# Seven more weight chunks of a three-block transformer done as seven half-size products instead of eight

## The reference, cut to what matters

```
# block one
proj = x @ w_in_a;  u = gelu(proj[:, :768]);  gv = layer_norm(gelu(proj[:, 768:1536]));  qm = proj[:, 1536:]
mix = u * (w_s @ gv + b_s);   att = concat(mix, memory_attention(qm, mk, mv)) @ w_out_a
# block two
q = x @ w_in_b[:, :768];  k = x @ w_k_shared;  v = x @ w_v_shared
# block three
h = rmsnorm(x);  rq, rk, rv, rg, nq, nk, nv, xq, gates = split(h @ w_in_2)
# each expert block
y += ((silu(t @ w_gate[e]) * (t @ w_up[e])) @ w_down[e]) * gate[e]
```

## Time and profile before

| what | us |
|---|---|
| median of three runs | 1697.32 |
| profiled execution, its device time | 1697.71 |
| span of the profiled execution | 1696.0 |
| PE busy | 1648.3 (97%) |
| VectorE busy | 448.9 (26%) |
| ScalarE busy | 288.5 (17%) |

### The profile page before, as it was taken

The page is one execution under the profiler, slowest core; times in us unless marked ns, Lnnn a source line. Parts: engine busy times, 40 slices in busy tenths (PEclk is TensorE's granted clock), DMA queues, the critical chain, the costliest instruction groups (busy, mean ns, idle before and its releaser), DMA issues.

```text
span 1696.0 us, 20423 instructions
## 1 busy us (share of the span) xinstructions
PE 1648.3 (97%) x8806; PEld 940.5 (55%) x8806; DVE 448.9 (26%) x940; ACT 288.5 (17%) x584; POOL 62.4 (4%) x92
## 2 busy tenths in 40 slices
PE   9999999999899999999999999899999999999997
PEld 7784433433333685644344333348787888866654
DVE  1470000000000225300000000025266657722222
ACT  2301101101011222111011000012222122321212
POOL 4000000000000100000000000005000000000000
PEclk9999999999999999999999999999999999999999
DMA  9889999999999955999999999999254445699996
GB/s 335 324 323 375 429 427 428 427 428 428 425 426 428 386 200 216 354 427 428 427 429 426 428 427 427 428 406 330 95 199 149 151 147 198 251 401 425 425 424 284
DMA packets 88491, 597.46 MB, mean 352 GB/s; under 512 B 6104, under 2 KB 17104, under 8 KB 54208
## 3 DMA queue, kind: packets, MB, share of 16 engines
q1 hardware_dynamic: 84768, 586.30, 85.4%
q0 software_dynamic: 3616, 9.65, 1.8%
HBM read 594.88 MB, written 1.05 MB: 351 GB/s over the span
## 4 chain that ended last, share of the span: by engine, by line
PE 59%; issue 26%; DMA 12%; DVE 2%; POOL 1%; ACT 0%; POOLq 0%; DVEq 0%
PE psum L952 31%; PE psum L658 8%; DMA ring<-in_w_gate_dram 8%; PE psum L645 4%; DMA ring<-in_w_up_dram 4%; PE psum L935 3%; PE psum L602 3%; PE psum L1046 2%; PE psum L652 1%; PE psum L893 1%; PE psum L1085 1%; PE psum L1062 1%; POOL rstd L3339 1%; PE psum L780 1%; PE psum L594 1%
## 5 line engine op out<-in xcount | busy, mean ns | idle before, releaser
L952 PE MATMUL psum<-ring,xT 128*64 128x512 f32 (+1 forms) x2020 | 416.4, 560 | 29.5 <-DMA ring<-in_w_up_dram 11.2
L952 PEld LDWEIGHTS psum<-ring,xT 128*64 128x64 f32 x2020 | 144.5, 137 | 272.7 <-issue 243.8
L952 PE MATMUL psum<-ring,work 128*64 128x512 f32 x992 | 220.1, 593 | 0.8 <-DMA ring<-in_w_down_dram 0.7
L2615 DVE TENSOR_TENSOR work<-work,psum 128x512 f32<-128x512 f32 (+1 forms) x45 | 41.0, 910 | 573.9 <-PE psum L952 568.3
L952 PEld LDWEIGHTS psum<-ring,work 128*64 128x64 f32 x992 | 70.7, 137 | 136.6 <-issue 131.3
L645 PE MATMUL psum<-xT,ring 128*128 128x256 f32 x512 | 113.6, 380 | 0.0
L1925 ACT COPY work<-psum 128x512 f32<-128x512 f32 (+1 forms) x45 | 23.2, 515 | 488.9 <-PE psum L1062 488.9
L658 PE MATMUL psum<-ring,mkv 128*128 128x256 f32 x456 | 104.9, 380 | 0.0
L645 PEld LDWEIGHTS psum<-xT,ring 128*128 128x128 f32 x512 | 96.3, 190 | 13.8 <-issue 0.8
L658 PE MATMUL psum<-ring,xT 128*128 128x256 f32 x400 | 92.0, 379 | 0.3 <-issue 0.3
L658 PEld LDWEIGHTS psum<-ring,mkv 128*128 128x128 f32 x456 | 85.7, 190 | 11.8 <-DVE work L3188 0.3
(11 more groups left out here) (378 smaller groups left out, 1647.2 us busy)
## 6 DMA issues: line engine op xcount, KB each, us to landing
ring<-in_w_gate_dram SPq DMA_DIRECT2D x48, 2048.0 KB, 20.5
ring<-in_w_down_dram SPq DMA_DIRECT2D x48, 2048.0 KB, 22.1
ring<-in_w_up_dram SPq DMA_DIRECT2D x48, 2048.0 KB, 21.8
ring<-in_w_in_dram SPq DMA_DIRECT2D x16, 2048.0 KB, 11.4
ring<-in_w_exp_up_dram SPq DMA_DIRECT2D x15, 2048.0 KB, 19.1
work<-in_w_gate_dram SPq DMA_DIRECT2D x10, 2048.0 KB, 14.5
ring<-in_w_exp_down_dram SPq DMA_DIRECT2D x10, 2048.0 KB, 20.4
work<-in_w_exp_gate_dram SPq DMA_DIRECT2D x9, 2048.0 KB, 15.0
```

The source lines that it names most:

```text
L952: ins = pe.matmul(to[part * CAP:(part + 1) * CAP, 0:n], lhsT=lhsT, rhs=w[:, half * n:(half + 1) * n], start=first, stop=last)
L2615: dve.tensor_tensor(by_rows(h[:, 0:F], j), in_order(silu[:, 0:F], j), in_order(u_bank[:, 0:F], j), ALU.mult).then_inc(sem("h"), 1)
```

## The change

The tokens and weights of seven more chunks are multiplied with the seven products: `VALUES_A` (512 columns of `gv`) and `INNER_A` (512 columns of `u`) in block one, `QUERY_D` and `KEYS_D` in block two, `QUERY_X`, `QUERY_N` and `KEYS_N` in block three. The first is natural, the other six are turned (`TURNED`). A turned product is eight matmuls of 128 columns where a natural one is four of 256. Blocks one and two get token sums and a scratch block of their own. PE's, ScalarE's and VectorE's lists are laid out anew around them; the order of the weight stream on SyncE is the same. The norm of the second memory is moved behind the keys of block two. The decays are computed at the start of the second expert stage. The join of the cross attention is split into four tiles between other work. Lines that only name things anew are left out.

```
+        TURNED = (INNER_A, QUERY_D, KEYS_D, QUERY_X, QUERY_N, KEYS_N)
+        seven_scale = {QUERY_D: -HD ** -0.5, QUERY_X: -P ** -0.5, QUERY_N: -HD ** -0.5}
+            def partial(b, at, tokens, weights, first=False, turned=False):
+                for f in range(2 if turned else 0):
+                    for c in range(4):
+                        ins = pe.matmul(b[:, f * P:(f + 1) * P], lhsT=weights[:, c, f * P:(f + 1) * P], rhs=tokens[:, c, :], start=first and f == c == 0, stop=(c == 3), skip_group_check=True)
+                for c in range(0 if turned else 4):
                     ins = pe.matmul(b[:, at:at + 256], lhsT=tokens[:, c, :], rhs=weights[:, c, :], ...
...
             # PE, block one
             two_turned(w[:, :, 256:512], xT, DC, 0, "a", "qm")
+            gated_values = first(n + 1)
             freed[n] = nat(w[:, :, 0:256], xT, DC, 256, "a", "gv", pack=True); n += 1
+            second(gated_values)
             scores(att_0, 0, q, keys)
-            tile(w, xT, DC, 512, 0, "a", "gv")
+            sixth_to_fifth(gated_values)
             scores(att_0, 1, q, keys)
             turn_weights(att_0, 0)
-            freed[n] = tile(w, xT, DC, 512, 1, "a", "gv"); n += 1
+            third(gated_values)
+            freed[n] = fourth(gated_values); n += 1
+            inner = first(n)
             scores(att_0, 2, q, keys)
             turn_weights(att_0, 1)
-            two_turned(w, xT, DC, 0, "a", "u")
+            second(inner)
+            sixth_to_fifth(inner)
             scores(att_0, 3, q, keys)
             values(att_0, 0, v)
             turn_weights(att_0, 2)
-            freed[n] = two_turned(w, xT, DC, 1, "a", "u"); n += 1
+            third(inner)
+            freed[n] = fourth(inner); n += 1
             turn_weights(att_0, 3)
...
             # PE, block two
             scores(att_m, 0, q, keys)
-            two_turned(w, xT, DC, 0, "a", "qkv")
+            query = first(n)
             scores(att_m, 1, q, keys)
             turn_weights(att_m, 0)
-            freed[n] = two_turned(w, xT, DC, 1, "a", "qkv"); n += 1
+            second(query)
+            sixth_to_fifth(query)
...
             # PE, block three
+            query = first(n)
+            second(query)
             gate_0 = first(n + 1)
-            freed[n] = two_turned(w, xT, DC, 1, "a", "xa"); n += 1
+            second(gate_0)
+            sixth_to_fifth(query)
+            third(query)
+            freed[n] = fourth(query); n += 1
...
             # ScalarE, block one
+            keep_first_part(VALUES_A)
             weights(att_0, 0)
-            empty(gv[:, 0, 0:512], "gv", ACT.Gelu)
+            keep_part(VALUES_A, 1)
+            keep_part(VALUES_A, 2)
             weights(att_0, 1)
             turn_weights(att_0, 0)
-            empty(gv[:, 1, 0:512], "gv", ACT.Gelu)
+            last_part(VALUES_A, ACT.Gelu)
+            keep_first_part(INNER_A)
+            in_place(VALUES_A, ACT.Gelu, "gv")
...
             # VectorE, block one
+            sum_tokens(VALUES_A)
+            sum_weights(VALUES_A)
+            first_corner(VALUES_A)
             peaks(att_0, 0)
             normal(att_0, 0)
+            other_corner(VALUES_A, 3)
             peaks(att_0, 1)
             normal(att_0, 1)
+            other_corner(VALUES_A, 2)
+            sum_weights(INNER_A)
             peaks(att_0, 2)
             normal(att_0, 2)
+            first_corner(INNER_A)
+            other_corner(INNER_A, 3)
             peaks(att_0, 3)
             output(oT[:, 0, :])
             normal(att_0, 3)
-            dve.wait_ge(S("gv_a"), 3)
+            dve.wait_ge(S("gv_a"), 4)
+            dve.wait_ge(S("last_part"), VALUES_A + 1)
+            other_corner(INNER_A, 2)
             layer_norm(halves(gv, SGW), gv, SGW, 0, (S("prm0_in"), 32))
...
             # VectorE, block two
+            sum_tokens(QUERY_D)
             peaks(att_m, 0)
+            sum_weights(QUERY_D)
             normal(att_m, 0)
-            rms_norm(mem2.__getitem__, mem2.__getitem__, prm[:, 0, 0, :], (S("prm0_in"), 48))
             peaks(att_m, 1)
+            first_corner(QUERY_D)
             normal(att_m, 1)
...
+            other_corner(KEYS_D, 2)
+            rms_norm(mem2.__getitem__, mem2.__getitem__, prm[:, 0, 0, :], (S("prm0_in"), 48))
...
-            expert_layer(1, count)
+            expert_layer(1, count_and_decays)
```

More of the change, by code:

```diff
@@ L1416, in _ @@
             turn_weights(att_m, 2)
-            freed[n] = two_turned(w, xT, DC, 1, "a", "qkv"); n += 1
+            second(keys_d)
+            sixth_to_fifth(keys_d)
             turn_weights(att_m, 3)
+            third(keys_d)
+            freed[n] = fourth(keys_d); n += 1
             two_turned(as_cols(n, 0, 256), xT, DC, 0, "a", "qkv")
@@ L1486, in xa_v @@
                 return mv2[:, k, h * P:(h + 1) * P]
-            second(gate_0)
             wait_made("xa")
+            seven_made(query)
             scores(att_x, 0, xa_q, xa_k)
-            sixth_to_fifth(gate_0)
-            scores(att_x, 1, xa_q, xa_k)
-            turn_weights(att_x, 0)
             third(gate_0)
@@ L1505, in _, with joined @@
             freed[n] = fourth(gate_1); n += 1
-            nq, nk = as_cols(n), as_cols(n + 1)
-            two_turned(nq, xT, DC, 0, "a", "na")
+            scores(att_x, 3, xa_q, xa_k)
+            query = first(n)
+            turn_weights(att_x, 2)
+            second(query)
+            sixth_to_fifth(query)
             turn_weights(att_x, 3)
-            b = bank("a", "na")
-            two_turned_part(nk, xT, DC, 0, b, range(0, 12))
+            third(query)
+            freed[n] = fourth(query)
+            keys = first(n + 1)
             values(att_x, 2, xa_v)
-            full("a", two_turned_part(nk, xT, DC, 0, b, range(12, 16)))
+            second(keys)
+            sixth_to_fifth(keys)
+            def joined(oT, at, half, t):
+                freed[at] = tile(as_rows(at)[:, :, half * 512:(half + 1) * 512], oT, 4, 512, t, "v", "joined")
             def join(oT, at):
-                w = as_rows(at)
                 for half in range(2):
-                    freed[at] = nat(w[:, :, half * 512:(half + 1) * 512], oT, 4, 512, "v", "joined")
+                    for t in range(TC):
+                        joined(oT, at, half, t)
             pe.wait_ge(S("att_o"), att_x.out(2))
-            join(W(XA["oT"], 4, T), n + 2)
+            oT_x = W(XA["oT"], 4, T)
+            joined(oT_x, n + 2, 0, 0)
+            third(keys)
+            freed[n + 1] = fourth(keys)
+            joined(oT_x, n + 2, 0, 1)
             qN, kN, vN = W(NA["qT"], 4, T), W(NA["kT"], 4, T), W(NA["v"], TC, 512)
@@ new lines, in add_product, with first_corner @@
+            def add_product(m, to, b):
+                if m in seven_scale:
+                    dve.scalar_tensor_tensor(out=to, in0=product_of(m, b), scalar=seven_scale[m], in1=to, op0=ALU.mult, op1=ALU.add).then_inc(S("corner"), 1)
+                else:
+                    dve.tensor_tensor(to, product_of(m, b), to, ALU.add).then_inc(S("corner"), 1)
+            def first_corner(m, between=None):
+                n, to, b = sevens[m], seven_to[m][0], bank()
+                dve.wait_ge(S("kept"), 3 * m + 1)
+                add_product(m, to, b)
+                if between is not None:
+                    between()
+                dve.wait_ge(S("weight_sums"), 4 * m + 3)
+                dve.tensor_tensor(block_of(n, 1, 0), block_of(n, 1, 0), sum_at(m), ALU.subtract).then_inc(S("weight_sums"), 1)
@@ L2655, in _, with other_corner @@
+            def other_corner(m, at):
+                if at == 3:
+                    dve.wait_ge(S("a_full"), cornered[m])
+                else:
+                    dve.wait_ge(S("part"), 4 * m + 4)
+                dve.wait_ge(S("kept"), 3 * m + at)
+                add_product(m, seven_to[m][at], RB["a"][(cornered[m] - 1) % BANKS])
             dve.memset(wr_mk[:], 0.0)
@@ L2934, in _, with join_first @@
-            join(XA["gate"])
+            peaks(att_x, 3)
+            sum_weights(QUERY_N)
+            normal(att_x, 3)
+            first_corner(QUERY_N)
+            other_corner(QUERY_N, 3)
+            other_corner(QUERY_N, 2)
+            sum_weights(KEYS_N)
+            output(oT[:, 2:4, :])
+            first_corner(KEYS_N)
+            gate_x = W(XA["gate"], TC, D)
+            def join_first(half, t):
+                cs = slice(half * 512, (half + 1) * 512)
+                dve.wait_ge(S("gate_a"), 2)
+                dve.tensor_tensor(comb[:, t, cs], bank(), gate_x[:, t, cs], ALU.mult).then_inc(S("joined_v"), 1)
```

292 lines of the change are left out of this document (164 added, 128 removed).

## The result

The changed kernel took 1716.81 us (median of 4 runs, 1715.33 to 1720.80), the kernel before 1697.62 us beside it. The ratio is 1.0118, with a 95% interval from 1.0106 to 1.0130. So it is slower by 19.2 us. The forecast was 1702.5 with a range up to 1707.5: the sign was right, the size wrong by a factor of nearly four. The profiled execution is the shortest of the four (1715.33, span 1713.3); against the span of 1696.0 before, the traces have 17.3 us to explain.

A forecast was written before the change was run, and what follows sets the result against it. Expert stages were taken as bound by their weight stream, passing on blocks one and two's lateness, block three by PE. Block one +5.25, two +2.0, three -2.1 gave +5.15 us: 1702.5, own range 1698.5 to 1706, 8-in-10 range 1692.5 to 1707.5.

The forecast's parts named there:

- three forecast pauses: PE waits for the third chunk's landing (2.95 us), before block one's out_second (4.0) and at block two's first softmax (3.9).
- one for one: Blocks one and two: a gain or loss by the block's end is carried whole to its expert stage's end.
- rival 2: The stream swallows blocks one and two's lateness, only block three's -2.1 us counts: 1695.2 us; chance 0.20.
- The PE work removed: All three blocks: VALUES_A saves 1.73 us, six turned chunks 5.8 at 1.835 a product, all seven 7.55.
- (a): Block one: third chunk, wanted earlier in first(n + 1), lands only at 34.3 us; PE stands for 2.95 us.
- (b): Block one: first(inner) waits 0.7 us for a bank, fifth twice 0.15 behind keep_part; 1.0 us in all.
- (c): Block one: gv's layer norm waits behind the last inner corner; 4.0 us of PE idle before out_second.
- Block two's first softmax: Block two: too little work covers the softmax and the weight sums; PE waits 3.9 us at turn_weights(att_m, 0).
- rival 3: The clock drops behind the three new pauses of 3 to 4 us, +2.0 each: 1704.5 to 1708.5; chance 0.15.
- Block three: Block three: products save 2.9 us, two relays cost 0.8 (0.6 and 0.2); -2.1 us in all.
- Rival 1: The waits are hidden on VectorE's list, only the chunk's landing stays: -4.6 us, 1692.7; chance 0.12.
- two decision points: out_second at most 13.1 us behind the inner columns' end (block one); no wait at turn_weights(att_m, 0) (block two).

The follow-up runs named there:

- four repairs: Changed kernel with bank wait split, gv chunk's first product behind packed tile, layer norm ahead of last corner, query tile between block two's scores: 1692.76 us, ratio 0.9975.
- fillers: Changed kernel with products of the identity laid into the four pauses of PE, no wait taken away: 1707.42 us, ratio 1.0054.
- split in the changed kernel: Changed kernel, but at block two's start PE waits for the second token tile's VectorE bank only ahead of that tile's transposes: 1710.52 us, ratio 1.0077.
- fifth repair: The four repairs, plus the second half's two sums of output weights on VectorE moved behind the first mixed tile: 1694.00 us, ratio 0.9984.

## Why the prediction was wrong

Two terms made the difference. The half clock behind the three forecast pauses was put at nothing and carried 7.3 us, and PE's wait at block two's start had no term and cost 6.4.

**What bounds the kernel, right.** The lateness of blocks one and two passed the expert stages but for 0.7 us each, which is within what executions differ by, so "one for one" held and rival 2 (the stream swallows it) fell. The single wait added to the kernel before shows it alone: 4.8 us of idle time and 2.3 of slow records at 570 us are +6.6 us at the end, more than 1,100 us later.

**The PE work removed, too small.** The turned product was priced at 1.835 us from two products that stand alone. Where turned products follow each other it is 1.785 (two from 1235.86 to 1239.43 take 3.57), and each change to another form adds about 0.1 us (two from 616.60 to the `scores` at 620.27 take 3.67). By starts, and without the pauses and the half clock, the turned chunks take 12.8 us for 13.9 in block one, 25.4 for 28.0 in two (four repairs) and 38.1 for 41.6 in three, so they save 7.3 where 5.8 was forecast. `VALUES_A` saves 1.4 where 1.73 was (12.6 for 14.0, four repairs). That is 1.2 us more in all, inside the bounds.

**Block one's waits, two right and one not there.** (a) The landing was forecast for 34.3 and came at 34.36, with PE idle for 2.42 us (forecast 2.95). (b) The 1.0 us for the bank and for `fifth` isn't in the trace: no pause is marked between the landing and 73.39, and `first(inner)` comes 1.87 us behind a product of 1.73. The inner columns ended at 73.39 (forecast 72.6); without the 1.7 us of half clock behind the landing they would have ended 0.9 ahead of the forecast, so that its nearness is luck. (c) The output product starts 17.6 us behind that end (forecast 17.1, before 13.1), and the pause is 4.02 us (forecast 4.0). The run with the norm ahead of the corner shows that their order was the cause.

**Block two's first softmax, right.** 4.07 us for 3.9.

**The term that was mis-sized: the half clock.** The text set it beside the sum ("The sum above has none: most short pauses of this trace leave the clock at 1.00") and gave rival 3 a chance of 0.15. This is the step that failed. "Most short pauses" counted pauses of about 1 us with those of 3, and I was adding pauses of 3 to 4. Of about such lengths the kernel before has three, all in its expert stages: 2.95 us at 428.8, 2.92 from 433.7 to 436.6 and 3.13 at 998.7. In its windows, the first two pauses lie in the first row and at the start of the second, the third in the third row, and the last row follows it:

```profile
428.00:436.00 8.00, 2.71 (x11) 0.57 (x8) 0.00 (x0) 0.59 (x1) 0.00 (x0) 1.00 1.00 419
436.00:442.00 6.00, 5.42 (x18) 2.33 (x19) 0.00 (x0) 0.00 (x0) 0.00 (x0) 0.72 1.02 433
997.00:1004.00 7.00, 3.87 (x19) 1.22 (x17) 0.00 (x0) 0.59 (x1) 0.00 (x0) 1.00 1.00 420
1004.00:1010.00 6.00, 6.00 (x31) 2.41 (x29) 0.98 (x1) 0.00 (x0) 0.00 (x0) 1.00 1.02 427
```

One in three was followed by a fall, at 2.0 us (the one from 433.7, which had another pause 2 us ahead of it). One in three alone put 2 us into the sum for three pauses, and 6 us into the range if all three fell, which is past the upper end that I gave. And even that share was too low. Over the eleven profiled executions (both kernels and the nine runs, read from their timelines of PE and their granted clocks), a fall followed 13 of 13 pauses of 4.0 us and more, 25 of 33 from 2.3 to 3.6 us, and none of those from 0.9 to 2.1. In the changed kernel, all three forecast pauses were followed by one; measured they carry 1.7, 2.9 and 2.7 us, and with the fourth 9.2 by the traces. The fillers gave 9.4, good to about 3 us, and in their profiled execution the first stretch was still slow; that the two figures are so close is partly luck.

**The term that was missing: block two's start.** Nothing in my steps had PE wait there. I took block two's start for untouched because the diff has no line in it. But a bank is handed out by a count that runs through the whole list, so that two takes more in block one change which bank a transpose gets 500 us later. It costs 6.3 us (split in the changed kernel) to 6.6 (put into the one before): 4.7 us idle, of which 4.5 are new, and the half clock behind them (1.9 us).

Both together: 5.15 + 7.3 (half clock behind the three forecast pauses) + 6.4 (4.5 and 1.9) = 18.9, less 1.2 for the products and 0.9 for the bank wait of (b) that isn't there, 16.8, against 17.3 in the traces. The 19.2 of the medians are 1.9 more, 1.5 of it because the profiled execution was the shortest of its kernel, and 0.3 because more device time lies around the span (2.0 us for 1.7). The chunk's landing fits the 1.5, but it wasn't tried.

**Block three, right.** -2.2 us where -2.1 was forecast, -1.6 by itself. Terms missed there in opposite directions. The products save 3.5 us where 2.9 was forecast. Two pauses of 0.47 and 0.52 us stand where 0.8 was counted for both relays. And changes between forms, which had no term, cost some 0.4: one chunk of 32 records of 512 columns is now in four pieces and takes 14.0 us instead of 13.8 (1239.43 to 1258.79 without what lies between; 1212.33 to 1226.16 before), and the transposes at 1224.40 take 0.64 instead of 0.44.

**The other side.** Rival 1 (faster, since the waits are hidden) had its two decision points in the right places. The version with the four repairs meets the second of them and comes close to the first, and is 4.8 us faster, where rival 1 had 4.6. That the figures agree is luck: rival 1 kept the wait for the landing, which this version doesn't have. Its PE work is about 8.8 us less; new pauses of 0.3 to 1.3 us, 3.8 us in all, take part of it back.

## What to carry to other kernels

Price a new pause of PE by its length and by what the rows behind pauses of that length lost, in as many traces as there are; here the second part was half the loss, and three pauses of one trace gave too low a share of falls. When a change adds takes of a resource that goes round by count (PSUM banks, ring places), look at every later wait whose target depends on the count, also where the diff has no line. And moving a step along an engine's list helps where it lands in idle time: the norm ahead of the corner used 3.38 us in which VectorE had waited for PE, while the two sums of weights behind the first mixed tile only moved the pause.

## What the runs showed of the hardware that I had not expected

- The granted clock fell behind each of the 13 pauses of 4.0 to 4.8 us in the eleven profiled executions and behind 25 of the 33 from 2.3 to 3.6 us (2.33, 2.42 and 2.50 among them; a 2.33, a 3.10 and a 3.13 were not followed by a fall). It never fell behind one of 0.9 to 2.1 us. Products with the identity kept it at 1.00 in the three pauses that they filled.
- It also fell where PE had no pause, in three of the eleven executions and always at one place of block three's end, behind small products of 20 columns. In the version with four repairs the six records of 512 columns at 1466.03 take 4.52 us, and 2.82 in the fifth repair, where the clock stays up (windows of the four repairs):

```profile
1460.00:1466.00 6.00, 6.00 (x49) 5.79 (x47) 4.11 (x6) 3.09 (x7) 0.54 (x1) 1.00 0.83 300
1466.00:1470.00 4.00, 4.00 (x8) 1.68 (x8) 3.46 (x16) 1.86 (x2) 0.00 (x0) 0.57 1.02 436
```

- Single gains added up: 24.4 us as four, 24.0 together, with a whole expert stage of 440 us between two of them.
- The landing of one and the same 2 MB chunk ended PE's wait at 34.4, 34.8, 34.9, 35.3 and 36.2 us in five profiled executions, with the same order of transfers ahead of it.
